# A convolution stage reordered on TensorE, VectorE and ScalarE, with its last weight split in quarters

## What is computed

```python
def conformer_conv(h, w_pw1, b_pw1, w_dw, b_dw, ln_g, ln_b, w_pw2, b_pw2):
    a = h @ w_pw1 + b_pw1
    u = a[..., :D_MODEL] * jax.nn.sigmoid(a[..., D_MODEL:])
    u = lax.conv_general_dilated(u, w_dw[:, None, :].astype(u.dtype), window_strides=(1,),
                                 padding=[(CONV_WIDTH - 1, 0)],
                                 dimension_numbers=('NWC', 'WIO', 'NWC'),
                                 feature_group_count=D_MODEL) + b_dw
    uf = u.astype(jnp.float32)
    mu = jnp.mean(uf, axis=-1, keepdims=True)
    var = jnp.mean(jnp.square(uf - mu), axis=-1, keepdims=True)
    u = ((uf - mu) * lax.rsqrt(var + EPS) * ln_g + ln_b).astype(h.dtype)
    return jax.nn.silu(u) @ w_pw2 + b_pw2

def swiglu(h, wg, wu, wd):
    return (jax.nn.silu(h @ wg) * (h @ wu)) @ wd
```

## Time and profile before

| | |
|---|---|
| median of the runs | 1261.8 us (1261.38 and 1261.8; a third at 2071.19) |
| the profiled execution | 1262.12 us, of which 1260.0 are its span |
| PE busy | 1226.8 us, 97% |
| DVE, ACT busy | 711.7 us (56%), 590.9 us (47%) |
| mean granted TensorE clock | 0.993 of full speed |
| PE idle in 392 to 420 us | 9.4 of 28 us, granted clock 0.82 |
| chain that ended last | PE 90%, DVE 5%, ACT 3% |

### The profile page before, as it was taken

How to read it: one execution, slowest core, us unless ns; L and a number is a source line. 1 busy time by engine, 2 the same in 40 slices (tenths; PEclk the granted TensorE clock), 3 DMA queues, 4 the chain that set the end, 5 groups by cost and what they waited for, 6 DMA issues and landing times.

```text
span 1260.0 us, 13744 instructions
## 1 busy us (share of the span) xinstructions
PE 1226.8 (97%) x5630; PEld 1008.0 (80%) x5630; DVE 711.7 (56%) x787; ACT 590.9 (47%) x674; POOL 39.7 (3%) x43
## 2 busy tenths in 40 slices
PE   7999999999997999999999999999999999999997
PEld 5776888888876788888888888888888878888885
DVE  6556755544667664544565454555477665554452
ACT  6554644454534554344454434455334444544441
POOL 2300000000110000000000000000000000000000
PEclk9999999999999899999999999999999999999999
DMA  8432476545341355545455544654554453645530
GB/s 328 152 109 79 156 275 218 188 179 186 149 167 67 134 201 182 180 177 196 167 206 195 185 180 173 261 196 167 200 193 142 140 193 136 228 175 197 181 137 33
DMA packets 32319, 220.65 MB, mean 175 GB/s; under 512 B 3729, under 2 KB 4129, under 8 KB 6530
## 3 DMA queue, kind: packets, MB, share of 16 engines
q1 hardware_dynamic: 32258, 219.79, 48.3%
HBM read 218.72 MB, written 1.05 MB: 174 GB/s over the span
## 4 chain that ended last, share of the span: by engine, by line
PE 90%; DVE 5%; ACT 3%; issue 1%; POOL 1%; DMA 0%; SPq 0%; POOLq 0%; DVEq 0%; ACTq 0%
PE ps L235 28%; PE ps L237 28%; PE ps L236 28%; PE ps L240 3%; PE ps L243 3%; DVE wlo L213 1%; ACT whi L206 1%; POOL st L356 1%; DMA raw<-in_w 0%; ACT xh L323 0%; DVE AR L1233 0%; DVE AR L1237 0%; ACT AR L1245 0%; DVE AR L1363 0%; POOL AR L611 0%
## 5 line engine op out<-in xcount | busy, mean ns | idle before, releaser
L213 DVE TENSOR_TENSOR wlo<-raw,whi 128x2048 fp32r<-128x2048 f32 x199 | 456.8, 2296 | 366.3 <-ACT whi L206 366.0
L206 ACT CAST whi<-raw 128x2048 fp32r<-128x2048 f32 x199 | 380.0, 1911 | 260.6 <-PE ps L237 260.6
L235 PE MATMUL ps<-whi,xh 128*128 128x512 f32 x1120 | 446.7, 399 | 6.5 <-DVE wlo L227 2.7
L237 PE MATMUL ps<-whi,xl 128*128 128x512 f32 x1120 | 438.6, 392 | 0.0
L236 PE MATMUL ps<-wlo,xh 128*128 128x512 f32 x1120 | 438.0, 391 | 0.0
L235 PEld LDWEIGHTS ps<-whi,xh 128*128 128x128 f32 x1120 | 211.1, 189 | 52.8 <-issue 3.8
L237 PEld LDWEIGHTS ps<-whi,xl 128*128 128x128 f32 x1120 | 211.2, 189 | 45.5
L236 PEld LDWEIGHTS ps<-wlo,xh 128*128 128x128 f32 x1120 | 211.6, 189 | 41.4
L235 PE MATMUL ps<-whi,yh 128*128 128x512 f32 x480 | 189.6, 395 | 1.4 <-DVE yl L1401 1.1
L237 PE MATMUL ps<-whi,yl 128*128 128x512 f32 x480 | 188.0, 392 | 0.0
L236 PE MATMUL ps<-wlo,yh 128*128 128x512 f32 x480 | 187.8, 391 | 0.0
(11 more groups left out here) (165 smaller groups left out, 582.4 us busy)
## 6 DMA issues: line engine op xcount, KB each, us to landing
raw<-in_w SPq DMA_DIRECT2D x199, 1024.0 KB, 4.8
raw<-in_w SPq DMA_DIRECT2D x4, 256.0 KB, 5.9
raw<-in_w SPq DMA_DIRECT2D x2, 512.0 KB, 7.5
AR<-in_b_pw SPq DMA_DIRECT2D x1, 1024.0 KB, 7.0
AR<-in_gate_bias SPq DMA_DIRECT2D x1, 1024.0 KB, 7.0
out<-AR SPq DMA_DIRECT2D x2, 512.0 KB, 2.6
AR<-in_dft SPq DMA_DIRECT2D x1, 864.0 KB, 9.0
AR<-in_rmask SPq DMA_DIRECT2D x1, 768.0 KB, 8.6
```

The costliest lines, as they stand in the source:

```text
L206: e.copy(whi[:, v % S, :], raw[:, v % R, :]).then_inc(*sig.up("hi", v))
L213: e.tensor_tensor(wlo[:, v % S, :], raw[:, v % R, :], whi[:, v % S, :].bitcast(F32), ALU.subtract).then_inc(*sig.up("lo", v))
L235: e.matmul(o, ah, bh, start=start, stop=False, skip_group_check=skip)
L237: return e.matmul(o, al, bh, start=False, stop=stop, skip_group_check=skip)
```

## The change

- pw1: VectorE's gate is cut in three (`vector_glu_sum`, `_product`, `_low`), and the pieces are interleaved between the two halves, with the weight remainders `lo` put behind them. A sum now also waits for the remainder of the same half one j earlier.
- Forward 0 and 1 move half a j later on TensorE (between the two units of t = 1), inverse 0 moves behind all of pw1, and forward 2 moves ahead of inverse 1.
- The split of c = 1 gets buffers of its own: `SH`, laid over `sil` and `hid`, which the stage doesn't use, and `two`. Inverse 2 gets banks 6 and 7 of its own (`conv_bank`), so the norm of a half reads three banks with three operations (512, 256, 256 columns) in place of two.
- The tail of VectorE: the norm of t = 0 comes ahead of the statistics of t = 1; the remainder of unit u + 9 (pw2's second) is cut in quarters and moved from pw1's last part to places in the tail.
- ScalarE's calls move with them: `hi` ahead of the split of c = 0, c = 1 ahead of the gate of (3, 1).

Numbers of instructions stay the same on TensorE; VectorE has five more.

```diff
+        SH = nc.alloc_sbuf_tensor_at("SH", [P, 4, 256], F32R, offset=nc.sbuf_base - 4 * 14080 - 4 * 1024)
...
+        def lo_quarter(e, q, v, k):
+            q.wait_ge(*sig.at("hi", v))
+            if v >= S:
+                q.wait_ge(*sig.at("used", v - S))
+            cols = slice(UC // 4 * k, UC // 4 * k + UC // 4)
+            e.tensor_tensor(wlo[:, v % S, cols], raw[:, v % R, cols], whi[:, v % S, cols].bitcast(F32),
+                            ALU.subtract).then_inc(*sig.up("lo", v) if k == 3 else sig.up("lo_quarter", v, k))
...
+        second = ((SH[:, 0, :], SH[:, 1, :]), (SH[:, 2, :], SH[:, 3, :]), (two[:, 0, :], two[:, 1, :]))
...
-        def vector_glu(e, q, j, t):
+        def vector_glu_sum(e, q, j, t):
             q.wait_ge(*banks.filled("pw1", j, t))
+            if j:
+                q.wait_ge(*sig.at("u_lo", j - 1, t))
             q.wait_ge(*sig.at("ld_bp1", 0))
             q.wait_ge(*sig.at("rstd", "mix1", t))
             e.scalar_tensor_tensor(out=glu[:, t, :], in0=ps[4 + t][:, :], scalar=rstd[:, t:t + 1],
                                    in1=bp1[:, 512 * j:512 * j + 512], op0=ALU.mult,
                                    op1=ALU.add).then_inc(*banks.empty("pw1", j, t))
+
+        def vector_glu_product(e, q, j, t):
             q.wait_ge(*sig.at("glu_sig", j, t))
             e.tensor_tensor(glu[:, t, 0:256], glu[:, t, 0:256], glu[:, t, 256:512],
                             ALU.mult).then_inc(*sig.up("glu_out", j, t))
+
+        def vector_glu_low(e, q, j, t):
...
             at, n = CH[c]
-            c0 = 256 if c == 2 else 0
             src = (prod[:, 0, 0:n], prod[:, 2, 0:n], spec[0:65, 2, at:at + n])[m]
             rows = slice(0, KS[m])
-            return sh[rows, m, c0:c0 + n], sl[rows, m, c0:c0 + n], src
+            if c == 1:
+                return second[m][0][rows, :], second[m][1][rows, :], src
+            return sh[rows, m, 0:n], sl[rows, m, 0:n], src
...
+        def conv_bank(t, c):
+            return 6 + t if c == 2 else 2 * t + c
+
         def tensor_inverse(e, q, c):
             at, n = CH[c]
             for t in range(2):
-                b = 2 * t + at // 512
-                if c < 2:
-                    banks.take(b, "conv", t, at // 512)
-                    q.wait_ge(*banks.room("conv", t, at // 512))
+                b = banks.take(conv_bank(t, c), "conv", t, c)
+                q.wait_ge(*banks.room("conv", t, c))
                 for m in range(3):
                     q.wait_ge(*sig.at("freq_lo", c, m))
                     h_, l_, _ = freq_part(c, m)
                     rows = slice(0, KS[m])
-                    last = mm3(e, ps[b][:, at % 512:at % 512 + n], gh[rows, m, tcols(t)], gl[rows, m, tcols(t)], h_, l_,
-                               m == 0 and c < 2, m == 2, skip=True)
-                last.then_inc(*(sig.up("conv_part", t) if c == 1 else banks.full("conv", t, at // 512)))
+                    last = mm3(e, ps[b][:, 0:n], gh[rows, m, tcols(t)], gl[rows, m, tcols(t)], h_, l_, m == 0, m == 2)
+                last.then_inc(*banks.full("conv", t, c))
...
-            for half in range(2):
-                e.tensor_scalar(xn[:, t, 512 * half:512 * half + 512], ps[2 * t + half][:, :], mv[:, 2 * t:2 * t + 1],
-                                mv[:, 2 * t + 1:2 * t + 2], ALU.subtract, ALU.mult).then_inc(*banks.empty("conv", t, half))
+            for c in range(3):
+                at, n = CH[c]
+                e.tensor_scalar(xn[:, t, at:at + n], ps[conv_bank(t, c)][:, 0:n], mv[:, 2 * t:2 * t + 1],
+                                mv[:, 2 * t + 1:2 * t + 2], ALU.subtract, ALU.mult).then_inc(*banks.empty("conv", t, c))
...
-            b = (6, 4)[t] + half
+            b = (4, 6)[t] + half
             banks.take(b, "normed", t, half)
             q.wait_ge(*banks.room("normed", t, half))
-            q.wait_ge(*banks.emptied("conv", t, half))
+            for c in ((0,), (1, 2))[half]:
+                q.wait_ge(*banks.emptied("conv", t, c))
...
-                    if j == 2 and t == 0:
-                        tensor_forward(e, q, 0)
-                    if j == 3 and t == 0:
-                        q.wait_ge(*sig.at("gl", 0))
-                        tensor_inverse(e, q, 0)
-                        tensor_forward(e, q, 1)
+                        if j >= 2 and t == 1 and i == 0:
+                            tensor_forward(e, q, j - 2)
                 sig.alias("used", (u + 1,), "full5", ("pw1", j, 1))
             sig.alias("x_free", ("mix1",), "full5", ("pw1", 3, 1))
+            q.wait_ge(*sig.at("gl", 0))
+            tensor_inverse(e, q, 0)
+            tensor_forward(e, q, 2)
             tensor_inverse(e, q, 1)
-            tensor_forward(e, q, 2)
             tensor_inverse(e, q, 2)
...
                 scalar_glu(e, q, j, 0)
-                if j == 2:
+                hi(e, q, u + 2 * j + 4)
+                if j < 2:
+                    scalar_glu(e, q, j, 1)
+                elif j == 2:
+                    scalar_glu(e, q, 2, 1)
                     scalar_freq(e, q, 0)
-                if j == 3:
+                else:
                     scalar_freq(e, q, 1)
-                hi(e, q, u + 2 * j + 4)
-                scalar_glu(e, q, j, 1)
+                    scalar_glu(e, q, 3, 1)
                 hi(e, q, u + 2 * j + 5)
...
-            for j in range(3):
-                vector_glu(e, q, j, 0)
-                if j == 2:
-                    vector_products(e, q, 0)
-                    vector_freq(e, q, 0)
+            for j in range(2):
+                vector_glu_sum(e, q, j, 0)
+                if j:
+                    vector_glu_low(e, q, j - 1, 1)
+                vector_glu_product(e, q, j, 0)
+                if j:
+                    lo(e, q, u + 2 * j + 3)
+                vector_glu_sum(e, q, j, 1)
+                vector_glu_low(e, q, j, 0)
+                vector_glu_product(e, q, j, 1)
                 lo(e, q, u + 2 * j + 4)
-                vector_glu(e, q, j, 1)
-                lo(e, q, u + 2 * j + 5)
-            vector_glu(e, q, 3, 0)
+            vector_glu_sum(e, q, 2, 0)
+            vector_glu_low(e, q, 1, 1)
+            vector_glu_product(e, q, 2, 0)
+            lo(e, q, u + 7)
+            vector_glu_sum(e, q, 2, 1)
+            vector_glu_low(e, q, 2, 0)
+            vector_glu_product(e, q, 2, 1)
+            vector_products(e, q, 0)
+            vector_glu_low(e, q, 2, 1)
+            vector_freq(e, q, 0)
+            vector_glu_sum(e, q, 3, 0)
+            lo(e, q, u + 8)
+            vector_glu_product(e, q, 3, 0)
+            vector_products(e, q, 1)
+            vector_glu_low(e, q, 3, 0)
+            vector_glu_sum(e, q, 3, 1)
+            vector_freq(e, q, 1)
+            vector_glu_product(e, q, 3, 1)
+            vector_glu_low(e, q, 3, 1)
             for t in range(2):
                 vector_stats(e, q, t, 0)
                 vector_stats(e, q, t, 1)
-            vector_products(e, q, 1)
-            vector_freq(e, q, 1)
-            vector_glu(e, q, 3, 1)
-            for t in range(2):
-                vector_stats(e, q, t, 2)
             vector_products(e, q, 2)
             vector_freq(e, q, 2)
             for t in range(2):
-                vector_stats(e, q, t, 3)
-                vector_moments(e, q, t)
+                vector_stats(e, q, t, 2)
+            vector_stats(e, q, 0, 3)
+            vector_moments(e, q, 0)
+            lo_quarter(e, q, u + 9, 0)
             vector_normed(e, q, 0)
+            vector_stats(e, q, 1, 3)
+            vector_moments(e, q, 1)
+            lo_quarter(e, q, u + 9, 1)
+            vector_remainder(e, q, 0, 1)
             vector_normed(e, q, 1)
-            vector_remainders(e, q, 0)
+            lo_quarter(e, q, u + 9, 2)
+            lo_quarter(e, q, u + 9, 3)
+            for t, c in ((0, 3), (0, 5), (0, 7), (1, 1), (1, 3)):
+                vector_remainder(e, q, t, c)
             lo(e, q, u + 10)
-            vector_remainders(e, q, 1)
+            vector_remainder(e, q, 1, 5)
+            vector_remainder(e, q, 1, 7)
             lo(e, q, u + 11)
             u = U["pw2"]```

`lo(e, q, v)` is `lo_quarter` in one piece; `vector_remainder(e, q, t, c)` is one turn of the loop in the old `vector_remainders`; `vector_glu_low` is the last third of the old `vector_glu`. The line numbers of the changed kernel are 9 to 19 higher in these functions.

**VectorE in pw1.** Rows of before, from the sum of (0, 0) (line 1233) to the sum of (1, 0); `wlo<-raw,whi` is `lo`, `AR<-ps,st,AR` the sum, `AR<-AR` the product, `yl<-AR,yh` the remainder of u:

```order
L1233 SCALAR_TENSOR_TENSOR AR<-ps,st,AR 128x512
L1237 TENSOR_TENSOR AR<-AR 128x256
L1240 TENSOR_TENSOR yl<-AR,yh 128x256
L213 TENSOR_TENSOR wlo<-raw,whi 128x2048
L1233 SCALAR_TENSOR_TENSOR AR<-ps,st,AR 128x512
L1237 TENSOR_TENSOR AR<-AR 128x256
L1240 TENSOR_TENSOR yl<-AR,yh 128x256
L213 TENSOR_TENSOR wlo<-raw,whi 128x2048
```

21 lines of the change are left out of this document (10 added, 11 removed).

## The result

The changed kernel takes 1248.95 us (median of 4 runs, 1247.9 to 1249.23); the kernel before took 1261.59 us on the same chip. The ratio is 0.990, 95% interval 0.988 to 0.9919: 12.6 us less. That is inside the predicted range, 2 us under the forecast of 1251.0 and 1 us under the 1250 to 1252.5 that the forecast spans by itself. One of the four runs behind the 1261.59 took 2071.19 us; without it their median is 1261.38.

A forecast was written before the change was run, and what follows sets the result against it. TensorE, 97% busy, bounds the kernel; its convolution stage loses 18.1 of 99.98 us. Work 81.9, holes 4.55, slow starts 0.3 and half clock 2.2 give 89.0, 11.0 less: 1251.0 us, range 1248 to 1255.

The forecast's parts named there:

- Pw1: Start of the convolution stage: interleaved gates close three TensorE holes, the third at forward 0, 2.4 us.
- Inverse 2: Hole between forward 2 and inverse 2: 3.0 us shrinks to 0.8 because inverse 1, 2.1 us, lies over it.
- Holes together and the stage without half clock: Whole stage: holes left 4.55 us, slow starts 0.3, own work 81.9, so 86.8 us without half clock.
- What the clock costs: Tail of the stage: one half-clock stretch after the last three holes, between 1.6 and 3.0 us lost, 2.2 taken.
- The rival in which it stays up: No half clock in the stage, perhaps no power delay: 13.2 to 13.8 us less, 1248.6 us; chance 0.17.
- The norm's hole: Ahead of the first transposes: 2.0 us becomes 1.5, plus 0.6 for GpSimd's power delayed beside a quarter, 2.1 left.
- The first remainder's hole: Ahead of pw2's first matmul: was 1.2 us, 1.4 left, with statistics of t = 1 and a quarter ahead on VectorE.
- The second half of the norm: Between the norm's two transpose groups: a third operation for the third bank makes a new 0.25 us hole.
- The step on inverse 1: Hole ahead of inverse 1: 3.7 us closed by TensorE work now over c = 1's products and split; needs the buffers.
- pw1 does not change: Rival: in pw1 the gates meet the same lap after all, 2.4 us stay, 1253.5 us; chance 0.06.
- The rival of VectorE's tail: VectorE's tail queue is the new bound: another 1 us wait and longer half clock, 1254 us; chance 0.17.
- The base of the sum: Profiled execution of 1262.12 us less 11.0 gives 1251.1; 18.1 us lost in the stage is the most any order gives.

The follow-up runs named there:

- after: The changed kernel, against the kernel before: 1248.95 us where that took 1261.59, ratio 0.990; a second profile's run took 1249.25 us.
- the kernel with the quarters moved: Changed kernel with the first low-part quarter put behind the moments of t = 1, the second behind the norm of t = 1: 1248.36 us.
- The kernels without half clock: Changed kernel with unread matmuls in three holes, 1247.72 us; that with quarters moved, 1247.76; with one low part and all holes filled, 1246.05.
- the fillers: Matmuls nobody reads, 3, 8 and 5 put in the changed kernel's holes ahead of inverse 2, first transposes and first output product: 1247.72 us.
- the fastest kernel: Changed kernel with the low part of u + 9 in one piece and unread matmuls in stage holes and two places outside: 1246.05 us, ratio 0.9884.

## Why the prediction was right, and where it was not

**Right by its mechanism, step by step.**
- *Pw1*: three holes closed, 2.4 us; no bracket stands there in after, and undoing this part alone brings three back.
- *Inverse 2*: 0.8 us forecast, 0.92 measured; putting inverse 1 first brings the 2.1 us back.
- *Holes together and the stage without half clock*: 4.55 and 86.8 us forecast. By the brackets of after the holes are 4.11, but partly under transposes at half clock. At full clock, with the last two brackets (0.28 and 1.04) from the kernel with the quarters moved, they are 0.92 + 2.14 + 0.44 + 1.20 = 4.70, and the formula gives 86.9. The kernels without half clock have 86.93, 86.91 and 86.92.
- *What the clock costs*: 2.2 forecast, 2.2 measured by the fillers. *Stage*: 89.0 forecast, 89.31 measured. The 2.2 was taken between two rows, 1.6 and 3.0, so that it fits to a tenth is luck.
- *The clock falls once*: it did, behind the group of the last three holes. The rival in which it stays up did not happen. The Trainium skill, page "TensorE: Matmul & The Clock Gate", section "Why this matters for your kernels", advises only against idle gaps longer than any in after; the row of 0.57 stands against reading that as a safe limit.

**Right in sum, mis-sized in its terms.**
- *The norm's hole*, 2.1 forecast and 2.14 measured, is two errors that cancel. The path without a disturbance is 1.60 + 0.16 = 1.76 us, not 1.5; the power's delay is 0.38, not 0.6. The step took all of the quarter's rest as delay. But the power is issued 0.16 us after the quarter has begun, when 0.52 us are left, and ends 0.41 us after the quarter where it takes 0.55 alone: 0.14 us of it are not delayed. The earlier trace rows have the same 0.13: that `lo` had 2.12 us left, the power took 1.99 longer than alone. The Trainium skill, page "SBUF — State Buffer", section "Who interferes with whom", has a VectorE instruction with two SBUF inputs and a GpSimd one that reads SBUF contend for a port pair that is an exclusive lock, and the powers that end only behind the subtraction agree with that; what the delay costs depends on when the second one comes.
- *The first remainder's hole*: 1.4 forecast, 0.74 measured. Of the 0.66 us, 0.46 are transposes that ran at half clock and so lay over it; at full clock it is 1.20. The step had VectorE's queue as the longest path. With no quarter ahead of the remainder the hole is still 0.89 + 0.16 = 1.05 us, so most of it is SiLU and high part on ScalarE.
- *The second half of the norm*: 0.25 forecast. The 0.31 measured are at half clock too; at full clock it is 0.28 + 0.16 = 0.44.

**Wrong.**
- *The step on inverse 1* gave the 3.7 us to the new order of TensorE and said "That needs the buffers". The hole did close, but pw1's order closes it alone, in the kernel before with shared buffers. What the step missed is VectorE's lag. It comes to pw1 about 5 us late, laps of 6.15 us against TensorE's 5.44 never let it catch up, and the wait falls due at 397.65, 36 us behind the row at 361.19. The rival *pw1 does not change* was mis-sized for the same reason, since 2.4 us were all that it put at stake there: with pw1's order undone the stage was 3.4 us longer, and in the old tail the same edit was worth 8.3.
- *The rival of VectorE's tail* was put at 0.17 for margins of tenths. No output product of after waits for it beyond the holes named. But at full clock the second one already does (0.28 us in the fastest kernel), so there was no margin.
- *The buffers* pay 2.2 us, but at forward 2, not at inverse 1.
- *The base of the sum.* The prediction took 11.0 us from one profiled execution, 1251.1, and the profiled execution of after has 1249.2: 10.7 us came in the stage, and 2.2 at places that the change doesn't touch. Without those the median would have been near the forecast; with them it lies beside the 1248.6 of the rival in which the clock stays up, which did not happen. The medians differ by 12.6. The two profiles of the kernel before have stages of 99.81 and 102.66 us, against 89.15 and 89.17: 10.7 and 13.5 us. So the 18.1 us lost, given there as the most any order could win, was the loss of one execution, not of the program. That the difference of the medians lies between these two is seen; how often each pattern of the clock comes is not, from two profiles.

## What to carry to other kernels

An engine that comes late and whose laps are no shorter than those of the engine it feeds stays late: that costs little where its own waits stand and far more where the lag falls due. Before giving a later hole to a later edit, look how late the engine already comes to it. When holes of 1 to 4 us stand close together, count the half clock behind them as a cost of its own, and look at two executions before sizing it; shortening one hole, as moving the quarters does, earns nothing if the next wait behind it ends when it did. Busy time at half clock counts too much where it lies over a wait. As many unread matmuls as fit in the holes are a cheap test of what the clock really costs, here 4.0 and 6.8 us in two profiles of the kernel before and 2.2 in the changed one.

## What the hardware showed that I had not expected

- The granted clock is no function of the program: the same hole of 1.91 to 1.92 us near 1030 us was followed by half clock in four profiles and not in nine, and in the kernel before both came out. From the turn to the end it is 823.9 to 824.0 us in the four and 822.3 to 822.4 in the others.
- Unread matmuls in the holes are nearly free: 41 of them in the kernel before made it 5.5 us (3.4 to 7.7) faster, not slower, and with 16 in the changed kernel the first output product came no later.
- A bracket depends on the clock of the work before it: ahead of the first output product it reads 0.58 us behind transposes at half clock and 1.04 behind transposes at full clock, with the same 1.66 to 1.67 us between their starts.
- A power of one column on GpSimd takes 0.55 us alone and 0.93 beside a VectorE subtraction of 0.68 us, with the same 0.41 us behind the subtraction's end in both pairs.
